# A squared-ReLU MLP in split fp32: up and down projection by one level of Strassen

## The reference, cut to what matters

```
D_MODEL = 2048; SEQ = 512; D_FF = 8192
h = h + merged @ w_out[l]
hn = rms_norm(h, norm_mlp_g[l])
u = jnp.square(jax.nn.relu(hn @ w_mlp_in[l]))     # (512, 2048) @ (2048, 8192)
h = h + u @ w_mlp_out[l]                          # (512, 8192) @ (8192, 2048)
return rms_norm(h, norm_final_g)
```

## Time and profile before

| | |
|---|---|
| time of the two runs shown | 2651.81 and 2651.90 us, median 2651.86 us |
| profiled execution | one of these two runs; its span from first to last instruction is 2649.5 us, so 2.3 to 2.4 us lie around the span |
| PE | busy 2636.4 us, 100% of the span, 12436 matmuls |
| PEld | 2206.3 us, 83% |
| DVE | 1046.9 us, 40% |
| ACT | 766.4 us, 29% |
| POOL | 0.2 us |
| PE clock granted | nine tenths or more in all 40 slices, mean 0.999 |
| DMA | 265 MB, mean 100 GB/s |
| where the MLP lies | from 1243.1 us to the end |

### The profile page before, as it was taken

How to read it: one execution, slowest core, us unless ns; L and a number is a source line. 1 busy time by engine, 2 the same in 40 slices (tenths; PEclk the granted TensorE clock), 3 DMA queues, 4 the chain that set the end, 5 groups by cost and what they waited for, 6 DMA issues and landing times.

```text
span 2649.5 us, 30377 instructions
## 1 busy us (share of the span) xinstructions
PE 2636.4 (100%) x12436; PEld 2206.3 (83%) x12436; DVE 1046.9 (40%) x1475; ACT 766.4 (29%) x1105; POOL 0.2 (0%) x4
## 2 busy tenths in 40 slices
PE   9999999999999999999999999999999999999998
PEld 8898888888888888888888888888888888888886
DVE  5565555455333334334333223332233332333333
ACT  4445443345222223223222122221122221222222
POOL 0000000000000000000000000000000000000000
PEclk9999999999999999999999999999999999999999
DMA  7222222222333332432333333333333333333333
GB/s 246 92 82 81 84 88 91 84 88 80 96 95 96 98 99 96 143 110 89 96 96 115 99 97 96 95 96 99 99 96 96 96 95 98 100 97 95 96 96 111
DMA packets 211142, 265.11 MB, mean 100 GB/s; under 512 B 8496, under 2 KB 162240, under 8 KB 210384
## 3 DMA queue, kind: packets, MB, share of 16 engines
q1 hardware_dynamic: 210880, 263.36, 31.8%
q10 hardware_dynamic: 144, 0.02, 0.0%
HBM read 259.11 MB, written 4.24 MB: 99 GB/s over the span
## 4 chain that ended last, share of the span: by engine, by line
PE 98%; DVE 1%; DMA 0%; ACT 0%; issue 0%; SPq 0%; DVEq 0%; ACTq 0%
PE bank L1116 32%; PE bank L1118 32%; PE bank L1117 32%; PE bank L1221 1%; PE bank L1204 1%; DMA landing<-in_w_in 0%; PE bank L1123 0%; DVE at_lo L919 0%; DVE at_lo L725 0%; DVE stream L1008 0%; DVE w_lo L725 0%; DVE stream L1072 0%; ACT w_hi L453 0%; ACT at_hi L453 0%; PE bank L1131 0%
## 5 line engine op out<-in xcount | busy, mean ns | idle before, releaser
L725 DVE TENSOR_TENSOR w_lo<-landing,w_hi 128x1024 fp32r<-128x1024 f32 x448 | 548.9, 1225 | 1362.2 <-ACT w_hi L453 1362.0
L453 ACT ACTIVATE w_hi<-landing 128x1024 fp32r<-128x1024 f32 x448 | 475.0, 1060 | 1624.1 <-PE bank L1118 1619.8
L1116 PE MATMUL bank<-w_hi,xn_hi 128*128 128x512 f32 (+1 forms) x1536 | 565.9, 368 | 0.1
L1118 PE MATMUL bank<-w_hi,xn_lo 128*128 128x512 f32 (+1 forms) x1536 | 563.6, 367 | 0.0
L1117 PE MATMUL bank<-w_lo,xn_hi 128*128 128x512 f32 (+1 forms) x1536 | 563.5, 367 | 0.0
L1116 PE MATMUL bank<-at_hi,w_hi 128*128 128x512 f32 x1280 | 498.6, 390 | 0.2 <-DVE w_lo L725 0.2
L1118 PE MATMUL bank<-at_hi,w_lo 128*128 128x512 f32 x1280 | 498.0, 389 | 0.0
L1117 PE MATMUL bank<-at_lo,w_hi 128*128 128x512 f32 x1280 | 498.0, 389 | 0.0
L1116 PE MATMUL bank<-xn_hi,w_hi 128*128 128x512 f32 x928 | 367.3, 396 | 2.2 <-DVE w_lo L725 1.2
L1118 PE MATMUL bank<-xn_hi,w_lo 128*128 128x512 f32 x928 | 361.8, 390 | 0.0
L1117 PE MATMUL bank<-xn_lo,w_hi 128*128 128x512 f32 x928 | 361.4, 389 | 0.0
(11 more groups left out here) (106 smaller groups left out, 1253.0 us busy)
## 6 DMA issues: line engine op xcount, KB each, us to landing
landing<-in_w_mlp_in SPq DMA_DIRECT2D x128, 512.0 KB, 3.8
landing<-in_w_mlp_out SPq DMA_DIRECT2D x128, 512.0 KB, 3.8
landing<-in_w_in SPq DMA_DIRECT2D x72, 512.0 KB, 3.5
landing<-in_w_gate SPq DMA_DIRECT2D x64, 512.0 KB, 3.9
landing<-in_w_out SPq DMA_DIRECT2D x32, 512.0 KB, 3.8
landing<-in_w_branch_a SPq DMA_DIRECT2D x16, 512.0 KB, 3.3
landing<-in_w_branch_b SPq DMA_DIRECT2D x16, 512.0 KB, 3.3
x_rows<-in_x SPq DMA_DIRECT2D x4, 1024.0 KB, 13.3
```

The lines of the kernel that those rows point to most:

```text
L453: nc.scalar.activation(hi, landing[:, u % LAND, :], ACT.Copy).then_inc(unit_hi, 1)
L725: nc.vector.tensor_tensor(lo, landing[:, u % LAND, :], hi.bitcast(F32), ALU.subtract).then_inc(unit_lo, 1)
L1116: nc.tensor.matmul(dst, a_hi, b_hi, start=start, stop=False, **kw)
L1118: return nc.tensor.matmul(dst, a_lo, b_hi, start=False, stop=stop, **kw)
```

## The change: Strassen in both projections

One level of Strassen (in the form with fewer additions) replaces both MLP products. The operands are cut in two along both axes, seven products of sums of such blocks are made in place of eight, and the output blocks are sums of the seven.

What is new, by name:

- **All of the up projection comes first**, in 128 units `(s, v)`: `s` is one of 32 groups of 256 hidden features, cut in two of 128, `v` one of four slices of the input features. A unit is one DMA of 512 KB, three POOL instructions that make four more blocks out of four (`up_sums`), one ACT copy and one DVE subtraction of 1792 columns (`up_high`, `up_low`), and 7 x 2 x 3 matmuls that stream 256 tokens. The weights were rearranged on the host into `up_units` and `down_blocks`. The input is now kept as seven token forms of 256 columns for each of eight feature pairs (`form_hi`, `form_lo`); the sums in it are made by POOL.
- After the four units of an `s`, ACT copies the first product out and DVE mixes the seven products into four blocks in five instructions and applies ReLU and the square in a sixth (`hidden`). The result goes to DRAM (`hidden_rows`), unscaled by token; the token scale comes in at the end of down as a factor of each tile (`scale`).
- **The down projection** has 16 steps `m`: 8 chunks of 1024 hidden features, each in two steps that make 512 columns of either half of the output. A step is 14 pieces, two for each of the seven products: an ACT copy and a DVE subtraction of 1024 columns each, 12 matmuls of 512 columns. The weight sums of a step are 8 POOL additions of 1024 columns, made in place (`down_sum`). In every odd step but the last, POOL makes the 4 sums of the next chunk's activations, and ACT and DVE split its 7 forms. Each product is added by DVE, two tiles of 512 columns, to the residual (`add_product`).
- `spread_rms(1)`, `norm_block` for the second norm and the MLP's old `hidden` are gone. Buffers of the mixers, of the up part and of the down part lie over each other in SBUF, so the first loads of each part wait for the last use in the one before.

The core of the diff:

```diff
+KP = KB // 2
+FORMS = 7
+SUBS = D_FF // CB
+UP_UNITS = 4 * SUBS
+UP_ORDER = ([(0, 0), (0, 1), (1, 0), (1, 1), (0, 2), (0, 3), (1, 2), (1, 3)]
+            + [(s, v) for s in range(2, SUBS) for v in range(4)])
+UP_FORM = (0, 3, 5, 1, 4, 2, 6)
+CHUNKS = SUBS // 4
+STEPS = 2 * CHUNKS
+PIECES = 2 * FORMS
+RING, RAW_SLOTS, FORM_SLOTS = 4, 6, 10
+QUARTERS = (0, 2, 1, 3)
+PIECE_BLOCK = (0, 0, 0, 3, 1, 2, 0)
+FORM_ORDER = (6, 1, 2, 3, 5, 0, 4)
+FORMS_AT = {7: (6,), 8: (1,), 10: (2,), 11: (3,), 12: (5, 0), 13: (4,)}
+ADDED = (None, (1, 1, 0), (0, 1, 1), (0, 0, 0), (1, 1, 1), (0, 1, 0), (1, 0, 0))
...
+        up_raw01 = sb("up_raw01", [P, 2, 8, CB], F32, up_phase)
+        up_hi1 = sb("up_hi1", [P, FORMS, CB], F32R, up_phase)
+        up_lo1 = sb("up_lo1", [P, FORMS, CB], F32R, up_phase)
+        unused_squares = sb("unused_squares", [P, QC], F32, up_phase)
+        up_hi0 = sb("up_hi0", [P, FORMS, CB], F32R, up_phase)
+        up_lo0 = sb("up_lo0", [P, FORMS, CB], F32R, up_phase)
+        up_raw2 = sb("up_raw2", [P, 8, CB], F32, up_phase)
+        mix = sb("mix", [P, FORMS, CB], F32, up_phase)
...
+        down_raw01 = sb("down_raw01", [P, 2, 4, QC], F32, down_phase)
+        ring12 = sb("ring12", [P, 2, 2, 2 * QC], F32R, down_phase)
...
+            for n, (s, v) in enumerate(UP_ORDER):
+                if n < 2:
+                    sp.wait_ge(unit_lo, 4 * B4)
+                elif n == 2:
+                    sp.wait_ge(unit_used, 4 * B4)
+                else:
+                    sp.wait_ge(up_lo_done, n - 2)
+                sp.dma_start(up_raw[n % 3][:, 0:4, :].rearrange("p b n -> p (b n)"), up_units[s, v])\
+                    .then_inc(up_landed[n % 3], 16)
+                if n >= 6 and UP_ORDER[n - 6][1] == 3:
+                    store_hidden(UP_ORDER[n - 6][0])
...
+            def up_high(n):
+                act.wait_ge(up_summed, 3 * n + 3)
+                if n == 0:
+                    act.wait_ge(unit_used, 4 * (B3 + 6) + 4)
+                elif n == 1:
+                    act.wait_ge(unit_used, 4 * B4)
+                else:
+                    act.wait_ge(up_used, n - 1)
+                nc.scalar.activation(up_hi[n % 2], up_raw[n % 3][:, 1:8, :], ACT.Copy).then_inc(up_hi_done, 1)
...
+            def piece_high(i):
...
+                if i == 0:
+                    act.wait_ge(up_used, UP_UNITS - 1)
+                elif i < RING:
+                    act.wait_ge(up_used, UP_UNITS)
+                else:
+                    act.wait_ge(piece_used, i - RING + 1)
+                nc.scalar.activation(ring[i % RING][:, 0, :], raw_of(w)[:, 2 * h:2 * h + 2, :].rearrange("p k n -> p (k n)"),
+                                     ACT.Copy).then_inc(piece_hi, 1)
...
+            def up_low(n):
+                dve.wait_ge(up_hi_done, n + 1)
+                nc.vector.tensor_tensor(up_lo[n % 2], up_raw[n % 3][:, 1:8, :], up_hi[n % 2].bitcast(F32),
+                                        ALU.subtract).then_inc(up_lo_done, 1)
...
+            def hidden(s):
+                done = 5 * s
+                dve.wait_ge(up_used, up_place(s, 3) + 1)
+                dve.wait_ge(first_copied, s + 1)
+                if s:
+                    dve.wait_ge(hidden_ready, s)
+                q1 = first_term[:, s % 2:s % 2 + 1, :].broadcast_to([P, 2, CB])
+                fifth, seventh = up_products(s, 3, 4), up_products(s, 4, 5)
+                nc.vector.tensor_tensor(mix[:, 0:5:4, :], up_products(s, 1, 6, 4), q1, ALU.add).then_inc(mixed, 1)
+                dve.wait_ge(mixed, done + 1)
+                nc.vector.tensor_tensor(mix[:, 5:6, :], fifth, mix[:, 4:5, :], ALU.subtract).then_inc(mixed, 1)
+                nc.vector.tensor_tensor(mix[:, 6:7, :], seventh, mix[:, 4:5, :], ALU.add).then_inc(mixed, 1)
+                dve.wait_ge(mixed, done + 3)
+                nc.vector.tensor_tensor(mix[:, 1:3, :], up_products(s, 2, 7, 4), mix[:, 5:7, :], ALU.add)\
+                    .then_inc(mixed, 1)
+                nc.vector.tensor_tensor(mix[:, 3:4, :], fifth, mix[:, 6:7, :], ALU.subtract).then_inc(mixed, 1)
+                dve.wait_ge(mixed, done + 5)
+                if s:
+                    dve.wait_ge(hidden_stored, 16 * s)
+                nc.vector.scalar_tensor_tensor(out=hidden_out[:], in0=mix[:, 0:4, :], scalar=0.0, in1=mix[:, 0:4, :],
+                                               op0=ALU.max, op1=ALU.mult).then_inc(hidden_ready, 1)
...
+            def form_split_lo(c, f):
+                dve.wait_ge(split_form_hi, form_count(c, f))
+                if f or c:
+                    dve.wait_ge(block_summed, 4 * c + (4, 2, 3, 3, 4, 3, 1)[f])
+                k = places[c][f]
+                nc.vector.tensor_tensor(split_form[k][:, 0], raw_form[k], split_form[k][:, 1].bitcast(F32),
+                                        ALU.subtract).then_inc(split_form_lo, 1)
+            def piece_low(i):
+                m, j, h = i // PIECES, i % PIECES // 2, i % 2
+                dve.wait_ge(piece_hi, i + 1)
+                part = ring[i % RING]
+                raw = raw_of(4 * m + PIECE_BLOCK[j])[:, 2 * h:2 * h + 2, :].rearrange("p k n -> p (k n)")
+                nc.vector.tensor_tensor(part[:, 1, :], raw, part[:, 0, :].bitcast(F32), ALU.subtract)\
+                    .then_inc(piece_lo, 1)
...
+            def add_product(m, j):
+                n = m % 2
+                dve.wait_ge(piece_used, PIECES * m + 2 * j + 2)
+                if m == 0 and j == 1:
+                    dve.wait_ge(tile_added, 4 * TT)
+                    dve.wait_ge(scale_ready, 1)
...
+                for t in range(2):
+                    src = bank[:, down_bank(m, j) + t, :]
+                    if j == 0 and m < 2:
+                        ins = nc.vector.tensor_copy(first_sum[:, n, t, :], src)
+                    elif j == 0:
+                        ins = nc.vector.tensor_tensor(first_sum[:, n, t, :], first_sum[:, n, t, :], src, ALU.add)
+                    else:
+                        row, half, minus = ADDED[j]
+                        dst = x_tok[:, 2 * row + t, half * D // 2 + n * QC:half * D // 2 + (n + 1) * QC]
+                        ins = nc.vector.scalar_tensor_tensor(
+                            out=dst, in0=src, scalar=scale[:, minus, 2 * row + t:2 * row + t + 1], in1=dst,
+                            op0=ALU.mult, op1=ALU.add)
+                    ins.then_inc(evacuated, 1)
...
+                piece_low(i)
+                if i % 2 == 0 and i >= 4:
+                    g = i // 2 - 2
+                    add_product(g // FORMS, g % FORMS)
+                    if g % FORMS == 0 and g // FORMS >= STEPS - 2:
+                        add_first_sum(g // FORMS)
+                if m % 2 == 1 and m < STEPS - 1:
+                    for f in FORMS_AT.get(p, ()):
+                        form_split_lo(m // 2 + 1, f)
...
+            def up_sums(n):
+                pool.wait_ge(up_landed[n % 3], 16 * (n // 3) + 16)
+                raw = up_raw[n % 3]
+                add(raw[:, 4:6, :], raw[:, 1:4:2, :], raw[:, 0:1, :].broadcast_to([P, 2, CB])).then_inc(up_summed, 1)
+                pool.wait_ge(up_summed, 3 * n + 1)
+                add(raw[:, 6, :], raw[:, 4, :], raw[:, 3, :]).then_inc(up_summed, 1)
+                pool.wait_ge(up_summed, 3 * n + 2)
+                add(raw[:, 7, :], raw[:, 6, :], raw[:, 2, :]).then_inc(up_summed, 1)
+            form_sums(form_raw_a, 0, 4, 8, 0)
+            for n in range(UP_UNITS):
+                up_sums(n)
+                if n in (2, 3):
+                    k = 2 * (n - 2)
+                    form_sums(form_raw_b, k, k + 2, 14 + k, 4 + 2 * k)
...
+            def down_sum(m, dst, src, pieces, h):
+                if pieces:
+                    pool.wait_ge(piece_lo, PIECES * m + pieces)
+                total = raw_of(4 * m + dst)[:, 2 * h:2 * h + 2, :]
+                add(total, total, raw_of(4 * m + src)[:, 2 * h:2 * h + 2, :]).then_inc(down_summed, 1)
+            for f in (1, 2, 5, 4):
+                block_sum(0, f)
+            for m in range(STEPS):
+                landed(4 * m)
+                landed(4 * m + 1)
+                down_sum(m, 0, 1, 1, 0)
+                down_sum(m, 0, 1, 2, 1)
+                landed(4 * m + 2)
+                down_sum(m, 0, 2, 3, 0)
+                down_sum(m, 0, 2, 4, 1)
+                next_sum(m, 1, 1)
+                down_sum(m, 1, 2, 0, 0)
+                down_sum(m, 1, 2, 0, 1)
+                next_sum(m, 2, 2)
+                landed(4 * m + 3)
+                down_sum(m, 0, 3, 5, 0)
+                down_sum(m, 0, 3, 6, 1)
+                next_sum(m, 5, 3)
+                next_sum(m, 4, 4)
...
+            def up(n, s, v):
+                pe.wait_ge(up_lo_done, n + 1)
+                if v == 0 and s < 2:
+                    pe.wait_ge(block_raw, 12 + 4 * s)
+                elif v == 0:
+                    pe.wait_ge(mixed, 5 * (s - 1))
+                for j in range(FORMS):
```

(50 more changed lines are left out.)

803 lines of the change are left out of this document (476 added, 327 removed).

## The result

The changed kernel takes **2723.42 us** (two runs, 2723.25 and 2723.59) against 2651.86: 1.027 times as long, 95% interval 1.024 to 1.0299. It is slower by 71.6 us; I had forecast 114.9 less. The time lies between my rivals 1 (2680) and 2 (2739).

A forecast was written before the change was run, and what follows sets the result against it. PE was taken as the bound, by number and price of matmuls. From 2651.9 us, 139.9 less on PE plus 25 of small terms gave 2537 us; the case's range was 2517 to 2580, the 8-in-10 range 2515 to 2710.

The forecast's parts named there:

- rival 1: Down, up and joints: DVE instructions with two SBUF inputs and POOL sums exclude each other; 2680 us; chance 0.30.
- Rival 2: Down steps: DVE's additions from PSUM overlap POOL's sums only in part; 2739 us at 4 us a step; chance 0.13.
- By itself POOL is hidden at both ends: Up and down: POOL's sums hidden behind PE, at most 2.3 us of 5.04 a unit, 27.4 of 38.2 an odd step.
- tail: After the last matmul: two tiles are added and two squares follow before the scaling; 2 us more (0 to 5).
- odd steps: Seven odd steps of down: DVE's extra form splits leave a debt mostly covered by the ring; 5 us (0 to 20).
- x: Down: the us of DVE's additions from PSUM that overlap POOL's sums in each step; 4 gave 2739 us.
- PE, up at 0.1200 us a matmul: Up projection: 5376 matmuls of 256 columns take PE 645.1 us, 52.6 less than before.
- PE, down at 0.2271: Down projection: 2688 matmuls of 512 columns take PE 610.4 us, 87.3 less than before.
- mixing in up: Up, once in four units: DVE's 3.8 us mixing delays the next subtraction; 2 us for all 32 (0 to 16).
- joint output projection to up: Start of up: PE waits 2 us for the first load and splits, then 3 at each of two units; 8 us (2 to 12).
- joint up to down: Start of down: first and second weight blocks come late, at most 4 us each; 8 us (3 to 15).
- Rival 3: Up: a 256-column matmul costs its weight load's 0.188 us; 366 us more, 2903; chance 0.05 together with worse joints.

The follow-up runs named there:

- e5: The changed kernel with the weight sums of both projections one column wide (up from the fourth unit on), sums of forms kept: 2540.70 us, 0.9581 of before.

## Why the prediction was wrong

**The step that failed** is the one that costs POOL's sums at nothing: "By itself POOL is hidden at both ends." I compared POOL's own sum with PE's time (27.4 of 38.2 us) and DVE's own sum with PE's time (36.1 of 38.2), each by itself. They are one sum: in an odd step 21 x 1.136 + 12 x 2.30 = 51.5 us before the first addition, which is no longer hidden behind 38.1. The profile of before could not show this, since POOL did nothing in it, but I had written the case down as rival 1 and gave it 0.30 against 0.52. That weighting was the error behind it. The argument I had used against it, that ACT and DVE work on one buffer without a longer record, was about two other engines.

The changed kernel shows the turns one by one (POOL and DVE, start, length; ACT and PE left out):

```profile
2200.19 3.39 POOL L1379 TENSOR_TENSOR raw_form<-raw_forms 128x1024 f32<-128x1024 f32 x1
...
2201.24 3.42 DVE L1273 TENSOR_TENSOR down_form<-raw_form,down_form 128x1024 fp32r<-128x1024 f32 x1
...
2203.53 6.63 POOL L1376 TENSOR_TENSOR down_raw<-down_raw 128x1024 f32<-128x1024 f32 x2
...
2204.59 3.36 DVE L1282 TENSOR_TENSOR ring<-down_raw,ring 128x1024 fp32r<-128x1024 f32 x1
...
2207.87 1.40 DVE L1307 SCALAR_TENSOR_TENSOR stream<-bank,scale,stream 128x512 f32<-128x512 f32 x2
```

DVE's instruction of 2201.24 ends at 2204.66, 1.1 us after POOL's sum that ended at 2203.58; POOL's next two take 6.63 us where 4.6 are due. Each record holds the other engine's turn, 2.30 + 1.14 = 3.4 us. The third line also shows why such a record must not be read as work: the 1023 us that the page gives POOL hold DVE's turns, and DVE's 1713.7 hold POOL's.

The Trainium skill (SBUF — State Buffer, "Who interferes with whom") states this rule, and I had quoted it and left it at 0.30. The traces agree with it in each of its parts that they touch: two SBUF inputs against a reading POOL block each other, PSUM inputs (673 ns) and POOL's writes (1210 ns) do not. They add one thing to a hold that lasts for one instruction: across sixteen sums in a row DVE did not get a turn at all.

**The price of a POOL sum was right.** I took 2.28 us, eight times DVE's 128-column price; it is 2.30 from start to start, 2343 ns as a record. Nothing in that multiple is about POOL, so that it came so near is luck. The Trainium skill (GPSIMD Engine Reference, section 3.1) gives 4497 ns for 2048 columns; as an estimate from that page 1024 would be 2.25 us, and the trace is within 5% of it.

**Why rival 1 still came out 43 us too low.** Not because of the pair. It gave an odd step 53.1 us and an even one 38.2 + 2, 93.3 a pair; measured are 93.9. That is partly luck: it priced DVE's 35 subtractions by their records (1.225) and not by their distances (1.136), 3.1 us too much, and left room for 2 us and for PE's own time in the even step, while I took the additions from PSUM as wholly hidden and 8.1 of 18.2 us were not. Inside the pair it was wrong, 49.0 and 44.8 in place of 53.1 and 40.2, since debt is carried from the odd into the even step. The missing time lies around the pairs:

- The last two steps are 23 us over PE's time; rival 1 gave them 4. Six additions of the first product into the residual, once in each, had no term of their own in my sum. They have both inputs in SBUF, and they are the same instruction, 512 columns wide, as the ones that read PSUM (740 ns). First the changed kernel, then e5:

```profile
L1319 DVE SCALAR_TENSOR_TENSOR stream<-first_sum,scale,stream 128x512 f32<-128x512 f32 x12 | 22.5, 1939 | 0.1
L1319 DVE SCALAR_TENSOR_TENSOR stream<-first_sum,scale,stream 128x512 f32<-128x512 f32 x12 | 8.1, 747 | 0.1
```

  Beside POOL's sums the six last 11.2 us, and PE stands still for 9.1 and 6.5 us behind them, at piece 5 of each of the two steps; in e5 both steps take 38.1.
- The first step is 20.5 us over PE's time, against 10. The start of up (2.3 us later, the first two groups 18.9 over) is 21 us, against 8.
- The other 30 groups of up are 0.9 us over in the mean, 26 in all, against 16 and 2 for the mixing, and the tail is 6.4 us longer, against 2.

These come to 55 us; 10 that rival 1 kept in reserve for odd steps and joints and 2 that the kernel before spent on waits and spreading, and that I had left in, go off.

**Rival 2** had the form of the answer, additions that overlap only in part, but not its numbers: a pair by it is 109.3 - 2x, and 93.9 gives x = 7.7, where I had set 4. With 7.7 its total is 2680 as well, for the same reasons; that x = 5.0 would give 2723 means nothing. I had given that rival 0.13.

**The rest of the sum stood.** With the weight sums out of the loops (e5) each of its terms can be read:

| term | predicted | in e5 |
|---|---|---|
| PE, up at 0.1200 us a matmul | 645.1 | 32 x 20.16 = 645.1 |
| PE, down at 0.2271 | 610.4 | 16 x 38.08 = 609.3 |
| mixing in up | 2 | 0 |
| odd steps | 5 | 0 |
| joint output projection to up | 8 | 2.3 later start, first group 14.2 over: 16.5 |
| joint up to down | 8 | first step 9.5 over |
| tail | 2 | 6.4 |
| total | 2537 | 2540.7 |

The last column's rows come to 2543.3 on the base that I used; 2.1 of the difference are the waits and the spreading that I had left in (1397.4 against 1395.3). Rival 3 is out: 256-column matmuls kept their 0.120 us.

Two small terms were mis-sized. The **first joint**: the copies of forms wait for POOL's sums of them. ACT at the start of up in the changed kernel:

```profile
1259.62 3.29 ACT L763 ACTIVATE form_hi_b<-form_raw_b 128x1792 fp32r<-128x1792 f32 x2 [6.55 <-POOL form_raw_b L1376]
1272.76 3.29 ACT L763 ACTIVATE form_hi_b<-form_raw_b 128x1792 fp32r<-128x1792 f32 x2 [6.90 <-POOL form_raw_b L1376]
```

Twice ACT stands still for 6.5 to 7 us until POOL has four sums of forms, the second time with the sums of a unit ahead of them; I had allowed 3 us each. The **tail**: I looked at what is added, not at what stands ahead of it. The last additions of the changed kernel:

```profile
2705.36 0.16 DVE L909 TENSOR_REDUCE stat<-squares 128x2 f32<-128x8 f32 x1 [1.40 <-ACT unused_down L841]
...
2707.47 0.17 DVE L915 TENSOR_SCALAR stat<-stat 128x2 f32<-128x2 f32 x1
...
2708.27 0.75 DVE L1356 SCALAR_TENSOR_TENSOR stream<-stream,stat,gain_row 128x512 f32<-128x512 f32 x1
2708.93 1.40 DVE L1307 SCALAR_TENSOR_TENSOR stream<-bank,scale,stream 128x512 f32<-128x512 f32 x2
```

PE's last matmul starts at 2706.07; the additions that need it start at 2708.93, since DVE's queue has the root of tiles 0 and 1 and the scaling of tile 0 before them. Before, that distance was 0.43 us: 2.4 of the 6.4 us. Of the other 4, 2.4 are the second tile's addition and square and the scaling of two tiles where one was left, and 1.5 the stores after them (5.9 us from the last scaling to the end, 4.4 before).

## What to carry to other kernels

Before giving POOL the sums of a loop, add them to DVE's instructions with two SBUF inputs as if one engine did both, and compare that one total with the bottleneck; POOL's and DVE's separate shares mean nothing once both are in it. Where the total is too long, DVE makes the sum itself in half the time that it would lose (2.30 against 1.14 us here). In these runs POOL was free help only beside DVE instructions that read PSUM or ACT's copies, or where it merely wrote. A record that grew while its engine's other kinds stayed the same (1225 to 1974 ns, with 744 staying at 740; 747 to 1939 for the same addition with both inputs in SBUF) points at a shared path rather than at a busy engine.
